# Seven block products instead of eight in 16 of the 22 pairs of the first FFN's input GEMM

## The chip, the core and the metric

The kernel runs on one core of a Trainium2 chip. The metric is device time in microseconds, the median over the runs of one kernel. TensorE does the matrix products into PSUM, VectorE (DVE) and ScalarE (ACT) work on SBUF and PSUM, GpSimd (POOL) on SBUF, SyncE (SP) issues most of the DMAs. The engines run their own queues and meet at semaphores.

## The reference

One inference step of one decoder layer: half-step SwiGLU, an attention and pooling block, half-step SwiGLU, each with adaLN modulation before it and a LayerNorm behind it. The change touches the first SwiGLU alone:

```python
def swiglu(u, w_in, w_out):
    a, b = jnp.split(u @ w_in, 2, axis=-1)
    return (jax.nn.silu(a) * b) @ w_out

def modulate(h, s):
    return h * (1.0 + scl[:, s]) + shift[:, s]

h = swiglu(modulate(x, 0), p['w_ffn1_in'], p['w_ffn1_out'])
x = layer_norm(ALPHA * x + 0.5 * gate[:, 0] * h, p['ln_gain'][0], p['ln_bias'][0])
```

The model width is 1024, the FFN width 2816, and there are 512 + 64 = 576 tokens. All is float32.

## The kernel before

**Layout.** Activations lie with features on the 128 partitions and the 576 tokens along the free axis, in 8 tiles (`XT`, the residual x; `UH` and `UL`, the modulated u). Every float32 operand is split into a high part in the matmul type fp32r (a copy on ACT) and a low part (a subtraction on DVE), and a product is three matmuls: high by high, high by low, low by high.

**The input GEMM of an FFN** makes 22 pairs of 128 columns, one of the a half and one of the b half of `w_in`. A plain pair is two chunks of 1024 x 128 weights. `product` (L344) runs one chunk: 8 feature tiles, 3 terms, 2 halves of 288 tokens, so 48 matmuls of 288 columns, and 96 a pair. ACT splits off the chunk's high part (`hi`, L259), DVE the low part (`lo`, L263), each into one of two slots; ACT takes the silu of a out of PSUM (L745), DVE multiplies by b (L763), ACT and DVE split the result into `HH` (L749) and `HL` (L769). Two chunks are on their way at a time.

**The seven-product form** is there before the change for 20 of the 22 pairs of the *second* FFN. The weights of a pair are seen as 2 x 2 blocks (a or b; lower or upper 512 features), and u as 2 x 2 blocks (lower or upper features; first or second 288 tokens). Seven products of sums of blocks replace eight. One product is 4 feature tiles, 3 terms, one half of the tokens: 12 matmuls (L1415), 84 a pair. The sums of weight blocks are four DVE subtractions and additions of 128x512 a pair (`block_s1` to `block_s4`, L1373 to L1390), the seven blocks are split by ACT (`block_hi`, L1364) and DVE (`block_lo`, L1369), and PSUM is read and added up by three ACT copies and three DVE additions a pair (L1434 to L1444, L1485 to L1493). The sums of u are made once (`factor_sums`, L1330, four instructions of 128x1152) and split once (`factor_hi` L1341, `factor_lo` L1345); two of the four split sums lie in `TB`, which shares its SBUF with `XT`, so x is spilled to DRAM (`spill`, L1532) and read back later (L991).

**What else runs in the first FFN.** The adaLN vectors of later stages are computed in five units beside the input GEMM. After each pair but the first two, TensorE runs two pieces (`ada_piece`, L1563) whose weights SP loads into `AW` (`ada_load`, L1555); a unit of eight pieces is copied out by ACT (`unit_copy`) and turned by TensorE (`unit_add`, L1577).

**Order.** Each engine's queue is written out by hand: `ffn_pe`, `ffn_act`, `ffn_dve` and `ffn_sp` in the first and second FFN. In the first, SP loads chunk after chunk, each when the slot's former chunk is split, and between them two `AW` loads a pair, each when TensorE has run the piece before the last in that buffer.

Of the kernel before, what the change touches and what calls it, by code (L numbers as in the profile page):

```python
# [7 lines left out]

# [5 lines left out]
F32 = mybir.dt.float32  # L14
# [9 lines left out]
KT = D // P  # L24
TP = 512
# [36 lines left out]
PHASES = [("setup", 0, 4, 4), ("ffn1_in", 2 * FT, FT, FT), ("ffn1_out", 3 * KT, 4, 4), ("ln0", 0, 1, 0),  # L62
# [22 lines left out]
def bucket_runs():  # L85
# [5 lines left out]
    return [int(np.argmax(b == k)) for k in range(NBKT)] + [len(b)]  # L91


def build(nc, x_prompt, x_sample, c_prompt, c_sample, cache_k_cmp, cache_v_cmp, cache_k_slc, cache_v_slc,
# [6 lines left out]
    with ExitStack() as ctx:  # L101
# [33 lines left out]
        STT = sb("STT", [TT, 9 * NT])  # L135
        ADS = RS[:, 0:2 * ACOL]
# [266 lines left out]
        def mod_buf(m, i):  # L403
            return U8[:, m, :] if i == 2 else T2[:, m % 2, :]

# [5 lines left out]
        def mod_hi(act, m, i):  # L411
            act.wait_ge(u32_ready, KT * i + m + 1)
            nc.scalar.activation(UH[:, m, :], T2[:, m % 2, :], ACT.Copy).then_inc(uh_done, 1)


        U8 = AR1[:, 8 * 2 * T:12 * 2 * T].rearrange("p (m t) -> p m t", m=KT)
# [204 lines left out]
        def ffn_pe(pe, i):  # L621
            a, b = f"ffn{i}_in", f"ffn{i}_out"

            def in_body(r, per, j0, first, unit=None):
                for j in range(j0, j0 + 4):
                    s = j % 2
                    if not first or j > 1:
                        pe.wait_ge(slot_free[s], SL0[a][s] + 1 + r * (per // 2) + j // 2)
                        if i == 2 and first and j == 2:
                            third_product(pe, a)  # L630
                            continue
                        product(pe, CH0[a] + r * per + j, (CH0[a] + j) % 2, s, 0, KT, UH, UL, True, True)
# [4 lines left out]
                    if unit is not None and s == 1:  # L637
                        k = (j - 4) % 8 - 1
                        ada_piece(pe, unit, k)
                        ada_piece(pe, unit, k + 1)  # L640
                        if k == 0 and first is None:
                            unit_add(pe, unit - 1, 5, T2[:, 1, 0:2 * P], unit * (2 * UCOL) - 2 * UCOL)
            in_body(0, 4, 0, True)
            if i == 1:
                in_body(0, 8, 4, False, 0)
                in_body(0, 8, 8, False, 0)
                with pe.Fori(1, FFN_UNITS) as r:
                    in_body(r, 8, 4, None, r)
                    in_body(r, 8, 8, False, r)
            else:  # L650
                seven_pe(pe)
                tokens_pe(pe)
                return
# [2529 lines left out]
```

## Time and profile before

| | us |
|---|---|
| median of 3 runs (1286.68 to 1290.34) | 1288.25 |
| the profiled execution, whole | 1289.31 |
| its span, first to last instruction | 1287.7 |
| TensorE busy (share of the span) | 1246.8 (97%) |
| VectorE busy | 697.8 (54%) |
| ScalarE busy | 512.5 (40%) |
| 20 pairs of the first FFN's input GEMM, pieces among them | 278.33 |
| 20 pairs of the second FFN's input GEMM (seven products) | 224.08 |

Times in the rows below are microseconds from the start of the span unless marked ns. Matmul rows overlap one another in the trace, so the mean duration of one (some 294 ns) is longer than the distance from one start to the next. That distance, a stretch of time by its count of matmuls, is what a matmul costs.

### The profile page before, as it was taken

The page shows a single profiled execution, that of the slowest core. Times are in us where ns is not written, and L with a number is a line of the kernel's source. Part 1 is how long each engine was busy: PE and PEld are TensorE (multiplying, and loading weights), DVE is VectorE, ACT ScalarE, POOL GpSimd, SP SyncE. Part 2 cuts the span into 40 slices and gives each one's busy share as a digit, 9 for nine tenths or more (in the row PEclk, how much of TensorE's full clock was granted, in tenths as well). Part 3 has the DMA queues.
Part 4 walks back from the last instruction along what each step waited for, and adds up shares of the span by engine and source line. Part 5 has one row for each costly group of instructions (what it writes and reads, how often), then busy time and mean ns, then how long its engine had stood idle before and what let it go on. Part 6 is the DMA issues. An engine that isn't in the chain of part 4 may idle for free.

```text
span 1287.7 us, 25082 instructions
## 1 busy us (share of the span) xinstructions
PE 1246.8 (97%) x9496; PEld 1116.2 (87%) x9496; DVE 697.8 (54%) x1244; ACT 512.5 (40%) x867; POOL 193.3 (15%) x379
## 2 busy tenths in 40 slices
PE   6999999999999999999989999999999999999997
PEld 3899999999899998999456666999999999978875
DVE  2522223223333357233468777578988888733466
ACT  3322222222211135343456655236556655533443
POOL 3000000000000022755085043022000000041000
PEclk9999999999999998999999999989999999999999
DMA  9535545545453224867453046623233333394463
GB/s 297 174 104 171 152 131 166 160 130 151 127 166 89 76 77 108 173 166 222 122 129 98 2 118 179 195 85 125 82 92 97 98 98 98 90 293 128 150 191 130
DMA packets 219628, 175.08 MB, mean 136 GB/s; under 512 B 47624, under 2 KB 198968, under 8 KB 219465
## 3 DMA queue, kind: packets, MB, share of 16 engines
q1 hardware_dynamic: 212641, 155.56, 41.7%
q0 software_dynamic: 6896, 18.35, 4.8%
q8 instruction: 52, 0.85, 0.3%
q14 instruction: 39, 0.32, 0.1%
HBM read 167.11 MB, written 10.99 MB: 138 GB/s over the span
## 4 chain that ended last, share of the span: by engine, by line
PE 87%; DVE 5%; ACT 4%; DMA 2%; issue 1%; DVEq 1%; SPq 0%; POOL 0%; ACTq 0%; POOLq 0%
PE ps L344 41%; PE ps L1415 16%; PE ps L1038 9%; PE ps L303 3%; PE ps L2896 2%; PE ps L2071 2%; PE ps L1563 1%; PE ps L2884 1%; ACT AR L2284 1%; DMA RAW<-in_w_ffn_out_dram 1%; PE ps L286 1%; PE ps L2088 1%; PE ps L2180 1%; PE ps L1614 1%; PE ps L425 1%
## 5 line engine op out<-in xcount | busy, mean ns | idle before, releaser
L263 DVE TENSOR_TENSOR WL<-RAW,WH 128x1024 fp32r<-128x1024 f32 x93 | 115.0, 1237 | 209.7 <-ACT WH L259 206.4
L344 PE MATMUL ps<-UH,WH 128*128 128x288 f32 x992 | 215.1, 297 | 1.0 <-DVE WL L263 1.0
L344 PE MATMUL ps<-UL,WH 128*128 128x288 f32 x992 | 210.9, 294 | 0.0
L344 PE MATMUL ps<-UH,WL 128*128 128x288 f32 x992 | 210.9, 293 | 0.0
L344 PEld LDWEIGHTS ps<-UH,WH 128*128 128x128 f32 x992 | 158.0, 188 | 7.4 <-issue 6.2
L344 PEld LDWEIGHTS ps<-UL,WH 128*128 128x128 f32 x992 | 159.4, 187 | 0.0
L344 PEld LDWEIGHTS ps<-UH,WL 128*128 128x128 f32 x992 | 158.4, 188 | 0.0
L259 ACT ACTIVATE WH<-RAW 128x1024 fp32r<-128x1024 f32 x93 | 97.9, 1054 | 143.4 <-PE ps L344 128.6
L1038 PE MATMUL ps<-WH,H 128*128 128x512 f32 x380 | 97.7, 398 | 0.8 <-ACT WH L1011 0.8
L574 POOL TENSOR_TENSOR AR<-AR 128x576 f32<-128x576 f32 x12 | 19.0, 1581 | 518.7 <-ACT AR L489 455.6
L1415 PE MATMUL ps<-TB,WH 128*128 128x288 f32 x480 | 96.8, 294 | 0.0
L1415 PE MATMUL ps<-UH,WH 128*128 128x288 f32 x320 | 94.1, 294 | 0.9 <-DVE RS L1489 0.9
L1415 PE MATMUL ps<-UL,WH 128*128 128x288 f32 x320 | 94.2, 294 | 0.0
L1415 PE MATMUL ps<-UH,WL 128*128 128x288 f32 x320 | 94.2, 294 | 0.0
L1038 PEld LDWEIGHTS ps<-WH,H 128*128 128x128 f32 x380 | 70.2, 188 | 18.4 <-ACT WH L1011 1.5
L1415 PEld LDWEIGHTS ps<-TB,WH 128*128 128x128 f32 x480 | 77.0, 187 | 0.0
L344 PE MATMUL ps<-HH,WH 128*128 128x288 f32 x338 | 72.2, 294 | 1.7 <-DVE HL L769 1.7
L344 PE MATMUL ps<-HL,WH 128*128 128x288 f32 x338 | 72.3, 294 | 0.0
L344 PE MATMUL ps<-HH,WL 128*128 128x288 f32 x338 | 72.0, 294 | 0.0
L1415 PE MATMUL ps<-TB,WL 128*128 128x288 f32 x240 | 70.9, 295 | 0.0
L1019 DVE TENSOR_TENSOR WL<-RAW,WH 128x1024 fp32r<-128x1024 f32 x28 | 34.9, 1247 | 50.5 <-ACT WH L1011 50.4
L1415 PEld LDWEIGHTS ps<-UH,WH 128*128 128x128 f32 x320 | 60.1, 188 | 1.1 <-DVE WL L1369 1.1
(445 smaller groups left out, 2335.0 us busy)
## 6 DMA issues: line engine op xcount, KB each, us to landing
RAW<-in_w_ffn_in_dram SPq DMA_DIRECT2D x58, 512.0 KB, 5.7
AW<-in_w_ada_dram SPq DMA_DIRECT2D x42, 512.0 KB, 4.3
RAW<-in_w_ffn_out_dram SPq DMA_DIRECT2D x36, 512.0 KB, 3.7
RAW<-in_w_ffn_in_dram SPq DMA_DIRECT2D x40, 256.0 KB, 2.9
AR<-in_w_ada_dram SPq DMA_DIRECT2D x7, 1024.0 KB, 11.4
RAW<-in_w_ffn_out_dram SPq DMA_DIRECT2D x16, 448.0 KB, 3.7
AR<-in_w_ada_dram SPq DMA_DIRECT2D x14, 512.0 KB, 5.9
RAW<-in_w_in_dram SPq DMA_DIRECT2D x28, 256.0 KB, 3.8
```

The source lines that it names most:

```text
L259: nc.scalar.activation(WH[:, slot, :], RAW[:, slot, :], ACT.Copy).then_inc(hi_done, 1)
L263: nc.vector.tensor_tensor(WL[:, slot, :], RAW[:, slot, :], WH[:, slot, :].bitcast(F32), ALU.subtract).then_inc(split_done, 1)
L286: mm = nc.tensor.matmul(ps[:, h, 0:HT], THIRD[ph][:, at + k * P:at + (k + 1) * P], R[:, k, h * HT:(h + 1) * HT], start=(k == 0 and q == 0) ...
L303: mm = nc.tensor.matmul(ps[:, 2 * s + h, 0:HT], W[:, w, k * P:(k + 1) * P], R[:, k, h * HT:(h + 1) * HT], start=(k == 0 and q == 0 and s n ...
L344: mm = nc.tensor.matmul(ps[:, 2 * uslot + h, 0:HT], W[:, wslot, k * P:(k + 1) * P], R[:, k0 + k, h * HT:(h + 1) * HT], start=(first and k ...
L425: mm = nc.tensor.matmul(ps[0:TT, bank, col + j:col + j + 1], src[:, j * TT:(j + 1) * TT], ONE[:, 0:1], start=True, stop=True)
L574: a = nc.gpsimd.tensor_tensor(sq[:, 0, :], sq[:, 0, :], sq[:, m, :], ALU.add)
L1019: nc.vector.tensor_tensor(WL[:, n % 2, :], raw_at(j)[0], WH[:, n % 2, :].bitcast(F32), ALU.subtract).then_inc(split_done, 1)
L1038: mm = nc.tensor.matmul(out, src, moving(h), start=(k == 0 and q == 0), stop=(k == FT - 1 and q == 2))
L1415: mm = nc.tensor.matmul(acc(bank), W[g % 4][:, k * P:(k + 1) * P], R[:, k, :], start=(k == 0 and q == 0 and i in (0, 1, 3)), stop=(k == HK ...
L2071: mm = nc.tensor.transpose(ps[:, 4 + g, k * P:(k + 1) * P], X[xslot(u, 2 * br + g)][:, k * P:(k + 1) * P], IDN[:, :])
L2896: mm = nc.tensor.matmul(ps[64 * g:64 * g + 64, 4 + kv, 0:NB * CS], WPHI[:, kv, l, :], KT8[kv][:, g, :, l % 8, l // 8:l // 8 + CS], start=( ...
```

## The change

Pairs 2 to 17 of the first FFN take the seven-product form; pairs 0 and 1, and 18 to 21, stay plain. The code of the second FFN becomes a form for both, with a record (`Seven`) of where each finds its buffers and counts.

- The modulated x, in float32, is no longer in a two-deep buffer (`T2`) but kept whole (`U1`), over the rows of x that have been turned already. The sums of u are made from it.
- x is spilled to DRAM as the stage begins and read back in its last four pairs.
- The split sums lie in `TB`, in parts of `HH` and `HL` that are filled last (18 to 21, hence 16 pairs), and in a new tile `FACX` of 128 x 1152.
- TensorE's two pieces follow each pair of seven products as they followed each plain pair. The unit's copy goes to `RS`, since `T2` holds block sums.
- ACT and DVE have the 16 pairs written out, in place of loops.

The core of the diff:

```diff
+        N1, N2 = 16, 20
+        SEVEN = (Seven(ffn=1, n=N1, ..., ring=0, raw=1, banks=((0, 1, 4), (2, 3, 7)),
+                       wb=(halves(RAW[:, 0, :]), halves(AR1[:, AR1N - WCH:AR1N])), xs=T2[:, 1, 0:BLK], u=U1,
...
         def mod_dve(m, i):
-            buf = T2[:, m % 2, :]
-            if m >= 2:
-                nc.vector.wait_ge(u_split, KT * UCNT[i] + m - 1)
+            buf = U1[:, m, :]
...
         def ffn_pe(pe, i):
-            if i == 1:
-                in_body(0, 8, 4, False, 0)
-                in_body(0, 8, 8, False, 0)
-                with pe.Fori(1, FFN_UNITS) as r:
-                    in_body(r, 8, 4, None, r)
-                    in_body(r, 8, 8, False, r)
+            in_body(0, True)
+            seven_pe(pe, SEVEN[i - 1])
...
+            pe.wait_ge(st_h, SEVEN[0].n - 1)
+            pe.wait_ge(st_sum, 3 * SEVEN[0].n - 3)
+            in_body(4, False)
+            in_body(8, False)
...
         def seven_pe(pe, V):
...
+                    if V.ffn == 1:
+                        unit_pieces(pe, r, p, not first)
...
         def ffn_sp(sp, i, w1, w2):
             if i == 1:
                 for j in range(2, 4):
-                    ffn_in_load(sp, 1, 0, 4, j, w1)
-                with sp.Fori(0, FFN_UNITS) as r:
-                    for j in range(4, 12):
-                        ffn_in_load(sp, 1, r, 8, j, w1)
-                        if j % 2 == 1:
-                            for k in (j - 5, j - 4):
-                                ada_load(sp, r, k)
+                    ffn_in_load(sp, 1, j, w1)
+                for s in range(2):
+                    sp.wait_ge(slot_free[s], 1 + KT // 2)
+                for k in range(2):
+                    ada_load(sp, 0, k)
+                for m in range(KT):
+                    sp.dma_start(XSP[:, m, :], XT[:, m, :]).then_inc(xsp, 16)
+                load_wb(sp, V, 1)
+                sp.wait_ge(split_done, CH0[a] + 5)
+                load_wb(sp, V, 0)
+                sp.wait_ge(split_done, CH0[a] + 6)
+                load_wa(sp, V, 0, 0)
+                load_wa(sp, V, 0, 1)
+                seven_sp(sp, V)
+                sp.wait_ge(st_split, 7 * V.n - 7)
+                ffn_in_load(sp, 1, 4, w1)
+                for k in range(6, 8):
+                    ada_load(sp, FFN_UNITS - 2, k)
+                sp.wait_ge(st_split, 7 * V.n - 1)
+                for j in range(5, 12):
+                    ffn_in_load(sp, 1, j, w1)
+                    if j % 2 == 1:
+                        for k in (j - 5, j - 4):
+                            ada_load(sp, FFN_UNITS - 1, k)
+                    if j == 5:
+                        sp.wait_ge(st_mm, 7 * V.n - 2)
+                    if j < 9:
+                        for m in (2 * j - 10, 2 * j - 9):
+                            sp.dma_start(XT[:, m, :], XSP[:, m, :]).then_inc(xsp, 16)
...
         def seven_sp(sp, V):
             for p in range(1, V.n):
+                q = V.done + p
+                sp.wait_ge(st_s13, 2 * q)
+                sp.wait_ge(st_s24, 2 * q - 1)
+                load_wa(sp, V, p, 0)
+                sp.wait_ge(st_split, 7 * q - 1)
+                load_wa(sp, V, p, 1)
+                if p + 1 < V.n:
+                    sp.wait_ge(st_split, 7 * q)
+                    load_wb(sp, V, p + 1)
+                if V.ffn == 1 and p + 1 < V.n:
+                    for k in (2 * (p % UNROLL), 2 * (p % UNROLL) + 1):
+                        ada_load(sp, p // UNROLL, k)
```

DVE's queue as the stage opens, before: the low part of the first FFN's third chunk stands right behind the last low parts of u.

```order
L408 TENSOR_TENSOR UL<-T,UH 128x576 [waits uh_done] x2
L263 TENSOR_TENSOR WL<-RAW,WH 128x1024 [waits hi_done]
L763 TENSOR_TENSOR T<-MU,ps 128x576 [waits hl_done,chunk_mm,slot_free0]
L769 TENSOR_TENSOR HL<-T,HH 128x576 [waits hh_done]
L263 TENSOR_TENSOR WL<-RAW,WH 128x1024 [waits hi_done] x2
```

The same place after; L1403 makes the sums of u, L1423 their low parts, L1466, L1471 and L1453 the sums of weight blocks, L1448 the low parts of blocks.

```order
L429 TENSOR_TENSOR UL<-AR,UH 128x576 [waits uh_done] x2
L1403 TENSOR_TENSOR AR<-AR 128x1152 x2
L286 TENSOR_TENSOR WL<-RAW,WH 128x1024 [waits hi_done]
L779 TENSOR_TENSOR T<-MU,ps 128x576 [waits hl_done,chunk_mm,slot_free0]
L286 TENSOR_TENSOR WL<-RAW,WH 128x1024 [waits hi_done]
L784 TENSOR_TENSOR HL<-T,HH 128x576 [waits hh_done]
L1403 TENSOR_TENSOR AR<-AR 128x1152 [waits tf_made] x2
L1423 TENSOR_TENSOR HH<-AR,HH 128x1152 [waits tb_hi]
L1466 TENSOR_TENSOR T<-RAW 128x512 [waits apre_full5]
L1471 TENSOR_TENSOR RAW<-RAW 128x512 [waits apre_full3]
L1448 TENSOR_TENSOR WL<-RAW,WH 128x512 [waits st_hi]
```

Two sums of u now stand ahead of the third chunk's low part, and two more sums, a low part and two block sums ahead of the first block's.

SP's queue at the same place, before: a loop of two chunk loads and two `AW` loads a pair (the bare `ISA` rows are its waits).

```order
L2961 DMA AW<-in_w_ada_dram 128x8x256
L240 DMA RAW<-in_w_ffn_in_dram 128x8x128 [waits split_done] x2
L862 UNCONDITIONAL_BRANCH
L862 ISA
L240 ISA [waits split_done]
L240 DMA RAW<-in_w_ffn_in_dram 128x8x128
L238 REGISTER_ALU
L240 ISA [waits split_done]
L240 DMA RAW<-in_w_ffn_in_dram 128x8x128
L1554 REGISTER_ALU
L1555 ISA [waits ada_mm]
L1555 DMA AW<-in_w_ada_dram 128x1024
```

And after (L1648 loads `AW`, L900 spills x, L1617 loads half an a chunk, L1621 a whole b chunk):

```order
L3055 DMA AW<-in_w_ada_dram 128x8x256
L263 DMA RAW<-in_w_ffn_in_dram 128x8x128 [waits split_done] x2
L1648 DMA AW<-in_w_ada_dram 128x1024 [waits ada_mm,slot_free1,slot_free0]
L1648 DMA AW<-in_w_ada_dram 128x1024 [waits ada_mm]
L900 DMA x_spill_dram<-XT 128x576 x8
L1621 DMA AR<-in_w_ffn_in_dram 128x8x128
L1621 DMA RAW<-in_w_ffn_in_dram 128x8x128 [waits split_done]
L1617 DMA RAW<-in_w_ffn_in_dram 128x4x128 [waits split_done]
L1617 DMA RAW<-in_w_ffn_in_dram 128x4x128
L1617 DMA RAW<-in_w_ffn_in_dram 128x4x128 [waits st_s24,st_s13]
L1617 DMA RAW<-in_w_ffn_in_dram 128x4x128 [waits st_split]
L1621 DMA RAW<-in_w_ffn_in_dram 128x8x128 [waits st_split]
```

The first loads of the seven-product stage stand behind two `AW` loads and the eight spills; from the second pair on, two `AW` loads that wait for TensorE's pieces (`ada_mm`) stand ahead of the next pair's first half chunk.

## Rows read from the trace of the kernel before

**Rows 1.** The page: busy time of each engine, share of the span, instructions.
```profile
span 1287.7 us, 25082 instructions
PE 1246.8 (97%) x9496; PEld 1116.2 (87%) x9496; DVE 697.8 (54%) x1244; ACT 512.5 (40%) x867; POOL 193.3 (15%) x379
```

**Rows 2.** Groups of PE: line, op, out<-in, shape, count, busy us, mean ns, idle before.
```profile
L344 PE MATMUL ps<-UH,WH 128*128 128x288 f32 x992 | 215.1, 297 | 1.0 <-DVE WL L263 1.0
...
L1415 PE MATMUL ps<-UH,WH 128*128 128x288 f32 x320 | 94.1, 294 | 0.9 <-DVE RS L1489 0.9
```

**Rows 3.** Windows: stretch, length, busy of PE, PEld, DVE, ACT, POOL, clock, DMA share, GB/s.
```profile
67.27:345.60 278.33, 278.33 (x2245) 264.00 (x2245) 79.27 (x80) 66.61 (x84) 0.00 (x0) 1.00 0.49 147
902.22:1126.30 224.08, 223.14 (x1684) 222.93 (x1683) 195.00 (x358) 133.77 (x260) 0.00 (x0) 1.00 0.33 94
```

**Rows 4.** Chain that ended last: start, length, what.
```profile
54.38 25.62 PE ps L344 x192
80.00 1.00 PE ps L1563 x16
81.00 12.89 PE ps L344 x96
...
912.99 205.44 PE ps L1415 x1548
```

**Rows 5.** Timeline of DVE as the first FFN opens: start, length, [idle before <-releaser].
```profile
49.59 1.60 DVE L408 TENSOR_TENSOR UL<-T,UH 128x576 fp32r<-128x576 f32 x2
53.01 1.22 DVE L263 TENSOR_TENSOR WL<-RAW,WH 128x1024 fp32r<-128x1024 f32 x1 [1.82 <-ACT WH L259]
```

**Rows 6.** Timeline of DVE and PE in the second FFN's opening.
```profile
887.57 2.62 DVE L1330 TENSOR_TENSOR AR<-AR 128x1152 f32<-128x1152 f32 x2
...
904.49 1.35 DVE L1345 TENSOR_TENSOR TB<-AR,TB 128x1152 fp32r<-128x1152 f32 x1
905.76 0.69 DVE L1369 TENSOR_TENSOR WL<-RAW,WH 128x512 fp32r<-128x512 f32 x1
...
912.39 0.45 DVE L1489 TENSOR_TENSOR RS<-RS,ps 128x288 f32<-128x288 f32 x1
```

**Rows 7.** Timeline of PE there.
```profile
912.99 0.37 PE L1415 MATMUL ps<-UH,WH 128*128 128x288 f32 x1 [0.94 <-DVE RS L1489]
```

**Rows 8.** Timeline of SP's DMA issues, first FFN's opening and the spill before the second.
```profile
31.51 26.87 SPq L240 DMA_DIRECT2D RAW<-in_w_ffn_in_dram  x4
58.64 1.08 SPq L1555 DMA_DIRECT2D AW<-in_w_ada_dram  x2
...
868.76 14.90 SPq L1532 DMA_DIRECT2D x_spill_dram<-XT  x8
```

**Rows 9.** The page's DMA issues: queue, count, KB each, us from issue to landing.
```profile
AW<-in_w_ada_dram SPq DMA_DIRECT2D x42, 512.0 KB, 4.3
RAW<-in_w_ffn_in_dram SPq DMA_DIRECT2D x40, 256.0 KB, 2.9
```

**Rows 10.** Windows as in rows 3: idle queue at the opening, mixed load and read-back, a slow-clock stretch.
```profile
46.00:50.00 4.00, 4.00 (x32) 3.95 (x32) 2.58 (x10) 1.25 (x3) 0.00 (x0) 1.00 0.00 0
864.00:868.00 4.00, 4.00 (x23) 3.20 (x23) 2.93 (x11) 1.36 (x2) 0.00 (x0) 0.50 0.72 214
1142.00:1156.00 14.00, 13.92 (x60) 11.25 (x61) 6.12 (x5) 4.28 (x5) 0.00 (x0) 1.00 0.97 322
```

**Rows 11.** Timeline of the setup's last adaLN products, which release `AW`.
```profile
44.77 1.05 PE L1637 MATMUL ps<-AW,CT 128*32 128x256 f32 x16
```

**Rows 12.** Waits in the second FFN's steady pairs: who, for whom, us in total, times, longest.
```profile
ACT WH L1364 <- DVE T L1373: 26.7, 18, 1.5
DVE WL L1369 <- ACT WH L1364: 20.9, 68, 0.3
```

More of the change, by code:

```diff
@@ L7 @@
 from contextlib import ExitStack
+from dataclasses import dataclass
 import numpy as np
@@ L24 @@
 KT = D // P
+HK = KT // 2
 TP = 512
@@ L91, in bucket_runs @@
     return [int(np.argmax(b == k)) for k in range(NBKT)] + [len(b)]
+@dataclass
+class Seven:
+    ffn: int
+    n: int
+    done: int
+    wa0: int
+    wb0: int
+    x0: int
+    ring: int
+    raw: int
+    banks: tuple
+    wb: tuple
+    xs: object
+    u: object
+    tf: object
+    fac1: tuple
+    fac4: tuple
 def build(nc, x_prompt, x_sample, c_prompt, c_sample, cache_k_cmp, cache_v_cmp, cache_k_slc, cache_v_slc,
@@ L788, in ffn_dve @@
[L788 to L801 removed]
+                factor_sums(V, 2, 3)
@@ new lines, in ffn_dve @@
+            block_lo(dve, V, 0, 1)
+            block_s2(dve, V, 0)
+            factor_lo(dve, V, 1)
+            factor_lo(dve, V, 2)
+            in_product(dve, 1, a, 3)
+            block_lo(dve, V, 0, 2)
+            block_lo(dve, V, 0, 3)
+            block_lo(dve, V, 0, 4)
+            block_s4(dve, V, 0)
+            in_low(dve, 1, 1)
+            seven_dve(dve, V)
+            for j in range(4, 12):
+                lo(dve, *split_args(*next_chunk(a, j))[:2])
+                if j % 2 == 1:
+                    in_product(dve, 1, a, j)
+                    in_low(dve, 1, pair_of(j))
@@ L1300, in blocks @@
+        def blocks(ar, first):
             flat = ar[:, :, :].rearrange("p s n -> p (s n)")
-            return [flat[:, ((q // 2 + RC) % 2) * WCH + (q % 2) * BLK:][:, 0:BLK] for q in range(4)]
-        WHB, WLB = blocks(WH), blocks(WL)
+            return [flat[:, ((q // 2 + first) % 2) * WCH + (q % 2) * BLK:][:, 0:BLK] for q in range(4)]
+        WHB, WLB = ([blocks(ar, V.ring) for V in SEVEN] for ar in (WH, WL))
+        RBLK = [halves(RAW[:, V.raw, :]) for V in SEVEN]
         tf_made, tb_hi, tb_split = sem("tf_made"), sem("tb_hi"), sem("tb_split")
-        LANDED = 16 + 16 * NPG
@@ L1470, in seven_dve @@
+                    act.wait_ge(st_h2, q)
+                    f = SP_F0 + p - 1
+                    dst = HH[:, f, :] if V.ffn == 1 else H2[:, f, 0:T]
+                    nc.scalar.activation(dst, EVH, ACT.Copy).then_inc(hh_done, 1)
+        def seven_dve(dve, V):
+            a, mm0, sm0 = f"ffn{V.ffn}_in", 7 * V.done, 3 * V.done
+            for t in range(7 * V.n + 1):
                 p, i = t // 7, t % 7
-                nxt = t + 3 < 7 * SP_N
+                q = V.done + p
+                nxt = t + 3 < 7 * V.n
```

587 lines of the change are left out of this document (297 added, 290 removed).

## The prediction

> **What bounds the kernel now.** I read the page's busy times first: TensorE is busy 97% of the span, VectorE 54%, ScalarE 40% [rows 1]. A busy PE is not yet a full one, so I then asked what PE waited for in the two FFN stages. In the groups of PE, the plain product (L344) has 1.0 us of idle time in front of 992 matmuls of one kind, the seven-product one (L1415) 0.9 us in front of 320 [rows 2]. The windows say the same: from 67.27 to 345.60 us, 20 pairs of the first FFN, PE is busy for all of 278.33 us at the full clock (1.00, so 2.4 GHz), while DVE works 79.27 and ACT 66.61 us [rows 3]. The stage is bound by the number of matmuls, and the helpers have room. So the saving is counted in matmuls, and the rest of the work is to find where the new form makes PE wait.
>
> **What a matmul costs.** The chain has 192 plain matmuls in 25.62 us, 0.1334 us each [rows 4]. The second FFN's 20 seven-product pairs take 224.08 us with one wait of 0.94 us in them: 223.14 / 1680 = 0.1328 us [rows 3, 7]. The two forms pay the same for a matmul, although the plain one runs each weight tile twice in a row and the other once. The Trainium skill ("TensorE: Matmul & The Clock Gate", Back-to-back issue gap) gives N/2.4 + 2.5 ns for one matmul, 122.5 ns at 288 columns. The trace disagrees, 133 ns; by the page's figure the next term would be an estimated 23.5 us.
>
> **Removed: 12 matmuls a pair.** 96 - 84 = 12, times 0.1334, is 1.60 us; 16 pairs make **-25.6 us**. Taken pair against pair it is 25.62 / 2 - 223.14 / 20 = 12.81 - 11.16 = 1.65, or -26.4. I take the first, since the shorter pair of the second FFN has no pieces after which PE starts anew (12.89 for the pair behind the pieces, against 12.81) [rows 4]. The pieces (1.00 us a pair) and the units' turns stay where they are, between pairs. A pair in the loop takes 278.33 / 20 = 13.92 us now and 12.3 after.
>
> **Helpers in steady pairs: nothing on the path.** The form asks DVE for 195.00 / 20 = 9.75 us a pair and ACT for 133.77 / 20 = 6.69 [rows 3]. In the second FFN that fits into 11.2 us without PE waiting; DVE's own waits there are short ones for ACT (0.3 us at the longest) [rows 12]. Here a pair has 12.3 us, DVE comes to 79%, and only `unit_copy` is new on ACT. The cover is 1.1 us better than where it already holds. If it were gone, each pair would lose what it is late.
>
> **SP's queue in steady pairs.** The next pair's first half chunk now stands behind two `AW` loads, which wait for the pieces of the pair before. Let a pair's first product start at T. The pieces end at T - 0.6 and T - 0.1, so the `AW` loads leave then and the half chunk at about T + 0.3. An `AW` load lands in 4.3 us and a half chunk in 2.9 [rows 9]; together with the two ahead of it (1.3 MB; at 214 to 322 GB/s [rows 10] 4.1 to 6.1 us) it lands by T + 3.5 to T + 5.5. DVE wants it for a block sum at about T + 6, behind four products' worth of work, and PE for the next pair at T + 12.3. Cost 0; PE has some 5 us in hand after the split (0.6 + 0.7 us, twice at most).
>
> **The opening, three terms.** (1) Two sums of u (2.62 us for two [rows 6]) now stand on DVE ahead of the third chunk's low part. DVE ends the low parts of u at 49.59 + 1.60 = 51.19 and idles until 53.01 for ACT [rows 5]. Of 2.62 us, 1.82 fall into this gap; the rest, **+0.8 us**, is on the path, since PE waits for this very instruction already (1.0 us) [rows 2]. (2) The first half chunk must come before about 62 us. `AW` is released at 44.77 + about 0.6 [rows 11], so its loads leave at about 45.4, 13 us earlier than now (58.64) [rows 8], onto an idle queue (0 GB/s from 46 to 50) [rows 10]. Behind them go 8 spills of 288 KB, two b chunks and the half chunk: 4.7 MB. At 322 GB/s, the rate of a stretch with weight loads and x read back [rows 10], they land by 60.1; at 214, the rate where spills begin, by 67.5. PE is done with the plain chunks at 55.2 + 12.8 = 68.0. The first rate costs nothing; by the second the first product starts 1 us late and DVE's queue behind it drags on, some 3 us in all. I take 0. (3) In the second FFN PE waits 0.94 us in its first pair [rows 7], for the middle addition at 912.39 [rows 6]: DVE had the split sums (1.35 us each), the blocks and the plain pair's end to do at once. Here one of these split sums is done before the first product, but ACT's block for it comes no earlier. Going down DVE's new list with these durations I find that addition ending at T + 10.0 where PE wants it at T + 9.6. Bounds 0 and 0.94, taken **+0.5 us**.
>
> **The close: nothing.** Chunk 4 is asked for in the last pair but one, and its split (1.0 + 1.2 us) starts when the last but two products is done, 3.2 us before the last ends, with 1.1 us of pieces behind it. The next chunk has 6.4 us more. Reading x back puts 2.4 MB among 4 MB of weights and 4 MB of `AW` loads in some 55 us, under 200 GB/s, where 322 have been seen [rows 10].
>
> **The sum.** -25.6 + 0.8 + 0 + 0.5 = -24.3 us. Against the profiled execution's 1289.31 that is 1265.0. This execution stands 1.06 us above the median of 1288.25, so the median after should be **1264.0 us**, 1.9% less. What a measurement of this kernel can tell from no change is about 0.3%, 4 us.
>
> **Rival 1: the opening chokes on the spill.** SP's single queue carries the 8 spills ahead of what PE needs next, and writing may be slower than reading. At half of 322 GB/s, 4.7 MB take 29 us, to 74.6; with split and DVE's list behind it PE loses 7 to 9 us, and, as the stretch at half clock (0.50) shows after a thin stretch of PE work [rows 10], perhaps 2 us more at 1.2 GHz. The time would be 1271 to 1275. For it: nothing in this trace has 8 spills at once; those seen came 1.9 us apart [rows 8]. Against: the idle queue and the 13 us of lead. The Trainium skill ("DMA: Bandwidth & Descriptors", Queues, rings and completion order) says that each DMA engine takes descriptors in ring order, which is what makes the spills stand ahead; what it would cost is the number above. Chance 14%.
>
> **Rival 2: a wait in every pair.** DVE and ACT pass blocks back and forth (26.7 us of ACT waiting for DVE in 18 pairs) [rows 12], now with other PSUM banks and the pieces between. If each pair lost 0.3 to 0.6 us, the time would be 1269 to 1274. Chance 8%.
>
> **Rival 3, the other side: the half chunk comes too late each time.** The mechanism is the SP order above: the `AW` loads wait for TensorE, the half chunk for them, and the next pair for the half chunk. It decides from a landing 5 us later than T + 5.5; from 6.6 us later (1.6 us a pair) the kernel is slower than before, at 8 us later 1288 + 16 x 1.4 - 1.5 = 1309. Loads that land 12 us after their issue would be needed; with a queue of 1.3 MB none of the kind is in the rows. Chance 2%.
>
> **Rival 4: the form saves less than it says**, because PE restarts cost more between short products. 7 waits a pair are there in the second FFN and cost nothing. Chance 4%, 1266 to 1270.
>
> **How the numbers follow.** The forecast, 1261.5 to 1268 with the bounds of its terms (-26.4 and no stall; 214 GB/s), has 72%. Up to 1273 the range takes in most of rivals 1 and 2 and leaves out some 12%. Faster by over 0.3% is 96%, within 0.3% is 2%, slower 2%.
>
> **What would show it.** In the trace after: 16 x 84 matmuls of the new form at 0.133 us from one start to the next; pairs of 12.3 us; the first plain chunk of `product` starting near 55.2 instead of 54.38; the eight spills leaving between 46 and 50 us and the first half chunk landing before 62; one wait of PE of about half a microsecond in the first pair, for DVE's middle addition; no wait for DVE or a load at the pair borders; the later stages unchanged but 24 us earlier. A wait at each border, or PE idle for more than 2 us between 55 and 85 us, would prove it wrong.

## The result, and the profile after

The changed kernel takes **1267.01 us** (median of 4 runs, 1266.38 to 1268.61), the kernel before beside it 1289.30 us (4 runs, 1286.68 to 1290.98): ratio **0.983**, 95% interval 0.981 to 0.985. Two further sets of runs of the same two kernels gave 1266.99 against 1290.07 and 1265.35 against 1290.92 us. Forecast were 1264.0 against a base of 1288.25, a ratio of 0.981. So the mechanism holds and the gain is 22 to 26 us where 24.3 were forecast. The profiled executions, which can be taken apart, are 22.9 us apart: 1289.31 before, 1266.38 after.

The page of the kernel after, against [rows 1]:

```profile
span 1264.4 us, 25031 instructions
PE 1221.5 (97%) x9304; PEld 1091.1 (86%) x9304; DVE 801.0 (63%) x1460; ACT 572.5 (45%) x1015; POOL 193.9 (15%) x379
```

192 matmuls fewer, which is 16 x 12, and DVE with 103 us more work than before. PE is as full as it was. The groups of PE, as in [rows 2], have idle times of 1.6, 0.9 and 0.4 us and no other in front of the products of the two input GEMMs:

```profile
L1500 PE MATMUL ps<-UH,WH 128*128 128x288 f32 x512 | 152.2, 297 | 0.9 <-DVE RS L1588 0.9
...
L367 PE MATMUL ps<-UH,WH 128*128 128x288 f32 x480 | 103.9, 297 | 1.6 <-DVE WL L286 1.6
...
L1500 PE MATMUL ps<-FACX,WH 128*128 128x288 f32 x64 | 18.9, 295 | 0.4 <-DVE RS L1588 0.4
```

The chain of work that ended last shows the stage pair by pair, as in [rows 4]. L367 is `product` now, L1500 the seven-product matmul, L1656 the adaLN pieces between the pairs:

```profile
55.84 12.95 PE ps L367 x96
...
78.69 1.82 PE ps L1500 x12
80.51 1.00 PE ps L1656 x16
81.51 11.32 PE ps L1500 x84
...
325.38 104.98 PE ps L367 x792
```

A seven-product pair behind pieces is 11.32 us, where a plain one was 12.89 [rows 4]; with the pieces 12.32. The windows of the first pair, of the 15 pairs that follow and of the plain pairs at the end (columns as in [rows 3]):

```profile
68.79:80.51 11.72, 11.36 (x88) 10.99 (x91) 11.04 (x18) 7.51 (x14) 0.00 (x0) 1.00 0.25 72
80.51:266.69 186.18, 186.18 (x1517) 174.98 (x1520) 144.97 (x251) 101.90 (x198) 0.00 (x0) 1.00 0.53 167
267.69:325.38 57.69, 56.00 (x453) 52.95 (x453) 16.95 (x20) 15.32 (x20) 0.00 (x0) 1.00 0.64 194
```

Over 15 pairs PE has not one gap, although DVE is busy 145 of 186 us (78%). The first pair has 0.36 us of idle time. The 57.69 us at the end hold the same code as before, between 290.64 and 348.32 in the kernel before 57.68.

**Where the 22.9 us come from** (23.3 of the span), by the start of the same instruction in the two traces. The third chunk's product starts 1.46 us later (54.38 [rows 4], 55.84). From there to the first product of the output GEMM before had 293.94 us, after 269.54: the stage is **24.40 us** shorter. From there to PE's wait in the second FFN's first pair it is 564.67 and 565.12 us, 0.45 more. The rest of the span is 0.8 us shorter, since one wait of PE of 0.8 us in the last stage is not there in this execution. 1.46 - 24.40 + 0.45 - 0.8 = -23.3 us of span.

### The profile page after: what moved, and what is told of

Same layout as the page of the kernel before. It is cut to its first block, busy times and chain, and to the rows that moved or that the text cites. A ratio compares the mean times of both kernels' runs of the same rounds, so it can differ in the third digit from the quotient of the medians.

```text
span 1264.4 us, 25031 instructions
## 1 busy us (share of the span) xinstructions
PE 1221.5 (97%) x9304; PEld 1091.1 (86%) x9304; DVE 801.0 (63%) x1460; ACT 572.5 (45%) x1015; POOL 193.9 (15%) x379
## 4 chain that ended last, share of the span: by engine, by line
PE 86%; DVE 6%; ACT 4%; issue 1%; DMA 1%; DVEq 1%; SPq 0%; POOL 0%; ACTq 0%; POOLq 0%
PE ps L1500 30%; PE ps L367 26%; PE ps L1101 11%; PE ps L326 3%; PE ps L2990 2%; ACT AR L2378 2%; PE ps L1656 2%; PE ps L2978 1%; PE ps L2165 1%; PE ps L309 1%; PE ps L1708 1%; DVE AR L2548 1%; PE ps L2274 1%; PE ps L2182 1%; PE ps L447 1%
## 5 line engine op out<-in xcount | busy, mean ns | idle before, releaser
L1500 PE MATMUL ps<-UH,WH 128*128 128x288 f32 x512 | 152.2, 297 | 0.9 <-DVE RS L1588 0.9
L1500 PE MATMUL ps<-UH,WL 128*128 128x288 f32 x512 | 150.9, 295 | 0.0
L1500 PE MATMUL ps<-UL,WH 128*128 128x288 f32 x512 | 150.6, 294 | 0.0
L286 DVE TENSOR_TENSOR WL<-RAW,WH 128x1024 fp32r<-128x1024 f32 x61 | 76.2, 1250 | 114.6 <-ACT WH L282 112.5
L1500 PE MATMUL ps<-TB,WH 128*128 128x288 f32 x736 | 148.7, 294 | 0.0
L1500 PEld LDWEIGHTS ps<-TB,WH 128*128 128x128 f32 x736 | 118.1, 188 | 0.0
L1448 DVE TENSOR_TENSOR WL<-RAW,WH 128x512 fp32r<-128x512 f32 x144 | 99.1, 688 | 28.5 <-ACT WH L1443 28.4
L1500 PE MATMUL ps<-TB,WL 128*128 128x288 f32 x368 | 108.7, 295 | 0.0
L367 PE MATMUL ps<-UH,WH 128*128 128x288 f32 x480 | 103.9, 297 | 1.6 <-DVE WL L286 1.6
L1443 ACT ACTIVATE WH<-RAW 128x512 fp32r<-128x512 f32 x144 | 90.3, 627 | 29.0 <-PE ps L1500 24.2
L367 PE MATMUL ps<-UH,WL 128*128 128x288 f32 x480 | 102.2, 294 | 0.0
L367 PE MATMUL ps<-UL,WH 128*128 128x288 f32 x480 | 102.2, 294 | 0.0
L1500 PEld LDWEIGHTS ps<-UH,WH 128*128 128x128 f32 x512 | 96.1, 188 | 6.1 <-DVE T L1575 3.7
L1500 PEld LDWEIGHTS ps<-UL,WH 128*128 128x128 f32 x512 | 96.1, 188 | 0.0
L1500 PEld LDWEIGHTS ps<-UH,WL 128*128 128x128 f32 x512 | 96.1, 188 | 0.0
L367 PEld LDWEIGHTS ps<-UH,WH 128*128 128x128 f32 x480 | 76.5, 188 | 3.0 <-issue 2.6
L367 PEld LDWEIGHTS ps<-UL,WH 128*128 128x128 f32 x480 | 77.0, 187 | 0.0
L367 PEld LDWEIGHTS ps<-UH,WL 128*128 128x128 f32 x480 | 76.7, 188 | 0.0
```

Source lines behind the costliest of these rows:

```text
L286: nc.vector.tensor_tensor(WL[:, slot, :], RAW[:, slot, :], WH[:, slot, :].bitcast(F32), ALU.subtract).then_inc(split_done, 1)
L367: mm = nc.tensor.matmul(ps[:, 2 * uslot + h, 0:HT], W[:, wslot, k * P:(k + 1) * P], R[:, k0 + k, h * HT:(h + 1) * HT], start=(first and k ...
L1443: nc.scalar.activation(WHB[V.ffn - 1][g % 4], block_raw(V, p, i), ACT.Copy).then_inc(st_hi, 1)
L1448: nc.vector.tensor_tensor(WLB[V.ffn - 1][g % 4], block_raw(V, p, i), WHB[V.ffn - 1][g % 4].bitcast(F32), ALU.subtract).then_inc(st_split, 1)
L1500: mm = nc.tensor.matmul(acc(bank), W[g % 4][:, k * P:(k + 1) * P], R[:, k, :], start=(k == 0 and z == 0 and i in (0, 1, 3)), stop=(k == HK ...
```

## The experiments

They are told by the question that they answer; all but two_terms (one term of each product left out) and extra_matmuls (some products counted twice) compute what the reference does. "The stage" is the time from the third chunk's first product to the first of the output GEMM, 269.54 us in the first trace of the changed kernel. It is compared rather than the span, since in the kernels that have one and the same code up to there, the third chunk's product starts anywhere between 54.70 and 56.44 us.

### Is the saving the matmuls, and nothing else?

**The same kernel again.**

> The changed kernel once more, to be compared with the others on one chip. All theories: about 1266 us in the profiled execution, 22 to 24 us under the kernel before; the pairs of seven products 12.3 us from one start to the next (84 matmuls in 11.3 and 1.0 for the pieces).

1266.99 us, ratio 0.9825 (0.980 to 0.985). Its stage is 325.16 - 55.62 = 269.54 us, the same to 0.01 us as in the first trace.

**Twelve pairs in the new form in place of 16.**

```diff
-        N1, N2 = 16, 20
+        N1, N2 = 12, 20
```

with eight plain pairs behind them instead of four.

> Seven products in 12 of the 22 pairs of the first FFN instead of 16, eight plain pairs behind them instead of four; the rest as in the changed kernel. If the gain is 12 matmuls a pair and the opening's cost is paid once, the time rises by 4 x 1.57 = 6.3 us over the changed kernel (12.89 us of matmuls in a plain pair, 11.32 in the other). If a good part of the loss against the plain sum came from something that grows with the number of pairs, the rise is below 5 us; if the transition costs more than the trace shows, it is above 7.

1273.03 us, ratio 0.9872 (0.985 to 0.989), 6.0 us above the changed kernel. The border between the forms in the chain:

```profile
205.86 11.32 PE ps L1500 x84
218.18 12.89 PE ps L367 x96
```

The stage is 331.87 - 56.05 = 275.82 us, 6.28 more: four times 1.57. The saving is in proportion to the pairs.

**The seventh product twice.** The pairs of the first FFN have 96 matmuls again, with all of the new form's work for DVE, ACT and SP.

```diff
-                        for k in range(HK):
+                        for k in [*range(HK)] * (2 if V.ffn == 1 and i == 6 else 1):
```

> In the first FFN the seventh product of every pair is run twice (its sum is then wrong, nothing else is changed), so that TensorE has 96 matmuls a pair as in the plain form, and ACT, DVE and SP all the work of the seven-product form. If only the number of matmuls matters and the helpers cost TensorE nothing, each pair takes 12.9 us and the pieces, and the time is that of the changed kernel + 16 x 1.60 = +25.6 us, that is 1 to 2 us above the kernel before. If the seven-product form gains by anything else, or loses by its helpers, the difference is not 25.6 but less or more by over 2 us.

1292.99 us, ratio 1.0027 (1.0002 to 1.0053), 26.0 us above the changed kernel. Its pairs in the chain:

```profile
83.36 12.90 PE ps L1500 x96
97.27 12.91 PE ps L1500 x96
```

With 96 matmuls a pair of the new form lasts as long as a plain one (12.89), and the gain is gone altogether. So the count of matmuls is the whole of the gain, and the new form's other work costs nothing in a steady pair. In all it costs some 2 us in this run: the stage is 351.03 - 55.41 = 295.62 us, 1.68 more than before the change (293.94), and the sums of u come on top with 0.55 (below). The 2.9 us between the medians are near what can be told from nothing. 26.08 us above the changed kernel's stage are a little more than 16 x 1.57, mostly because the first pair waits 1.05 us here where it waits 0.36 there; *The spill earlier* comes back to that.

### How much room do the helpers have?

**56 matmuls a pair**: high weights by low activations is left out of the first FFN's seven products.

```diff
                             for z, (W, R) in enumerate(((whb, rh), (whb, rl), (wlb, rh))):
+                                if V.ffn == 1 and z == 1:
+                                    continue
```

> In the first FFN's seven products the term high weights by low activations is left out (8 matmuls a product instead of 12, 56 a pair; the output loses that part). TensorE then needs 56 x 0.133 = 7.5 us and 1.0 for the pieces, 8.5 us a pair. If the helpers have the room that their busy times say (DVE 9.0 us of busy time a pair, with ends that overlap), they become the bound and a pair takes 8.7 to 9.7 us. If the hand-over between ACT, DVE and TensorE is already nearly as long as the pair, it stays above 11 us.

1236.58 us. The pairs are some 10.2 us, not 8.5 (56 x 0.1334 + 1.0). A window over a dozen pairs, and PE's waits in it (who, for whom, us in total, times, longest):

```profile
82.00:230.00 148.00, 134.38 (x1056) 116.68 (x1049) 135.82 (x244) 92.03 (x190) 0.00 (x0) 0.99 0.67 205
```

```profile
ACT WH L1443 <- DVE T L1453: 20.8, 14, 1.5
PE ps L1502 <- DVE RS L1590: 13.3, 14, 2.9
ACT WH L1443 <- DMA RAW<-in_w_ffn_in_dram: 12.2, 13, 2.9
```

DVE is busy 92% and PE waits in each pair for the middle addition (L1590 here, L1588 in the changed kernel): DVE's work with its hand-overs to ACT, and the half chunk's landing, do not go below 10.2 us. That lies between the two outcomes of the expectation (8.7 to 9.7, or above 11). Against 12.3 it leaves some 2 us a pair.

### What does the opening cost, and why?

**The sums of u later.** The two sums stand on DVE behind the third chunk's low part.

```diff
-            factor_sums(V, 0, 2)
             lo(dve, *split_args(a, 2)[:2])
...
             in_low(dve, 1, 0)
+            factor_sums(V, 0, 2)
             factor_sums(V, 2, 4)
```

> The two sums of u that stand ahead of the third chunk's low part on DVE are moved behind the fourth chunk's. By the theory (they cost 0.55 us at this place and nothing elsewhere), TensorE starts the third chunk 1.0 us after it is out of work, as in the kernel before, instead of 1.55, and DVE's later list still ends in time; the first pair of seven products keeps its wait of 0.3 to 0.5 us. If the sums only moved the lateness, the first seven-product pair waits longer by what the third chunk gains.

One run of 1265.91 us. PE's wait for the third chunk is 1.00 us again, as before the change [rows 2], against 1.55 in the changed kernel: so the sums on the path cost 0.55 us. But the stage is 325.66 - 54.87 = 270.79 us, 1.25 more: PE now waits 1.04 us for the middle addition in the first pair, where it had waited 0.36, and another 0.31 us for ACT earlier in the same pair. The work was not saved by moving it, only paid later; net it loses 0.7 us, and the total, which seems to say the opposite, is the setup's chance.

**The spill earlier**: the eight spills leave SP ahead of the `AW` loads, with a semaphore of their own.

```diff
+                for m in range(KT):
+                    sp.dma_start(XSP[:, m, :], XT[:, m, :]).then_inc(xsp1, 16)
                 for k in range(2):
                     ada_load(sp, 0, k)
-                for m in range(KT):
-                    sp.dma_start(XSP[:, m, :], XT[:, m, :]).then_inc(xsp, 16)
```

> The eight spills are issued before the two AW loads, which wait for the setup's last products, and count on a semaphore of their own. The first half chunk should land 2 to 4 us earlier and DVE's wait for it (1.2 us) go. TensorE's time should not change (within 0.2 us at the first product of the stage), since DVE is on time there without it; if the load's wait was part of the path, the first pair's wait of 0.4 us goes too.

One run of 1266.26 us. DVE's wait for the half chunk, 1.22 us in the changed kernel, is gone, and the stage is 324.56 - 55.01 = 269.55 us, no shorter at all. In the first pair PE waits 0.35 us as it did. In the changed kernel DVE's wait for the load lies in its slack: with the load early DVE idles 0.64 us instead, up to 68.03, 0.07 us after TensorE's last plain product of the opening ends, and only there the list that leads to the middle addition begins.

The slack was nearly used up, though, and extra_matmuls, which runs the same instructions up to there, shows the edge. First the changed kernel, where T, the end of the plain products, is 68.79, then extra_matmuls, where it is 68.36:

```profile
63.93 0.69 DVE L1471 TENSOR_TENSOR RAW<-RAW 128x512 f32<-128x512 f32 x1 [1.22 <-DMA RAW<-in_w_ffn_in_dram]
78.69 0.37 PE L1500 MATMUL ps<-FACX,WH 128*128 128x288 f32 x1 [0.36 <-DVE RS L1588]
```

```profile
64.25 0.69 DVE L1471 TENSOR_TENSOR RAW<-RAW 128x512 f32<-128x512 f32 x1 [1.51 <-DMA RAW<-in_w_ffn_in_dram]
78.95 0.37 PE L1500 MATMUL ps<-FACX,WH 128*128 128x288 f32 x1 [1.05 <-DVE RS L1588]
```

A landing at T - 4.9 us cost nothing, one at T - 4.1 cost 0.7. In the other traces with these sums ahead of the third chunk (double_spill and two_terms apart) DVE had the half chunk at T - 4.9 or before, and the wait is 0.35 to 0.38 us.

**The spill twice**, eight more writes of 288 KB into a second buffer, waited for as the first.

```diff
                 for m in range(KT):
+                    sp.dma_start(XSP2[:, m, :], XT[:, m, :]).then_inc(xsp2, 16)
+                for m in range(KT):
                     sp.dma_start(XSP[:, m, :], XT[:, m, :]).then_inc(xsp, 16)
```

> x is spilled twice as the stage opens, to two places in DRAM: 16 spills of 288 KB instead of 8, ahead of the first loads of the seven-product stage, and ACT waits for both. If the queue is what those loads wait behind, 2.36 MB more at about 350 GB/s shift the first half chunk by 6 to 8 us, from 63.9 to about 71, and TensorE stands still for 3 to 6 us before or in the first pair. If the spill is hidden anyway (rival), TensorE's waits stay at 0.4 us.

1273.47 us, one run. DVE and PE in its timeline, and the window of the first pair:

```profile
68.39 0.69 DVE L1472 TENSOR_TENSOR T<-RAW 128x512 f32<-128x512 f32 x1 [6.29 <-DMA RAW<-in_w_ffn_in_dram]
...
70.55 0.41 PE L1506 MATMUL ps<-UH,WH 128*128 128x288 f32 x1 [1.77 <-DVE WL L1454]
```

```profile
70.55:86.65 16.10, 14.39 (x101) 13.22 (x101) 15.24 (x23) 10.24 (x18) 0.00 (x0) 0.89 0.23 67
```

The half chunk lands at 69.1 in place of 63.9 us. The first product starts 1.8 us late, but the stage is 5.13 us longer (330.52 - 55.85 = 274.67): DVE, which had idled 6.3 us for the b chunk on the same queue (L1472 is the first block sum), then works through its list almost in one piece (15.24 of 16.10 us), and PE stands idle another 1.7 us, at a mean clock of 0.89. That mean is a fall to the lower level: PE had been idle for 1.77 us up to 70.55, and from 71.72 to 75.13 us the granted clock is 0.50 (1.2 GHz), with matmuls 0.24 us apart in place of 0.13. So the first 24 take 4.99 us where 24 x 0.134 are 3.2. A late start of 1.75, 1.35 more waiting than in the changed kernel and 1.8 for these 24 are 4.9 of the 5.13 us. That is rival 1, made to happen, with the "perhaps 2 us more at 1.2 GHz": it takes 2.3 MB more on the queue. Another 2 us of its 7 stand behind the stage, where nothing was changed: 1.45 between the output GEMM and the second FFN's first pair and 0.5 after it. They stay unexplained; one_copy (below) has 1.0 us more at the first of these places as well.

**All three at once**, and the low part of the second plain chunk's result (`in_low`, 0.75 us) moved behind the middle addition in both FFNs.

```diff
-                in_low(dve, 2, 1)
...
-            in_low(dve, 1, 1)
             seven_dve(dve, V)
...
                     nc.vector.tensor_tensor(EVP, EVP, acc(V.banks[p % 2][0]), ALU.add).then_inc(st_sum, 1)
+                    if p == 0:
+                        in_low(dve, V.ffn, 1)
```

> The changed kernel with three moves in its openings, nothing left out: the eight spills leave SP ahead of the AW loads; the two sums of u stand on DVE behind the third chunk's low part and the low part of the first half chunk's chunk; and in both FFNs the low part of the plain chunk that follows the seven-product opening (in_low for chunk 1) stands behind the middle addition of the first pair. Theory (DVE's queue in the first pair is what makes PE wait, and nothing else is late): the third chunk's wait falls from 1.55 to 1.0 us, the first-pair waits of 0.36 us (first FFN) and 0.93 us (second) go, so 1.3 to 1.9 us less in all and a profiled time of about 1265, with the setup's own spread of up to 0.9 us on top. Rival A (moving the sums alone cost 1.2 us in the first pair, since it put DVE behind for all that follows): the early spill does not give that back, the third chunk gains 0.55 us and the first pair loses about 1 us, and only the second FFN's 0.9 us remains as gain: 1266 to 1267. Rival B: the low part that was moved is now late itself and PE waits at the border of the first and second pair.

1266.26 us, ratio 0.982 (0.979 to 0.985), beside 1265.35 us of the changed kernel in the same set of runs: no gain. The stage is 324.22 - 53.48 = 270.74 us, as with the sums alone: the first half of rival A. Its other half, a gain of 0.9 us in the second FFN, did not come: the second FFN, where the moved low part was meant to take the wait of 0.93 us away, has it still:

```profile
887.43 0.37 PE L1499 MATMUL ps<-UH,WH 128*128 128x288 f32 x1 [0.94 <-DVE RS L1587]
```

DVE's timeline there tells why, first of the changed kernel, then of this one:

```profile
883.88 0.68 DVE L1459 TENSOR_TENSOR RAW<-RAW,T 128x512 f32<-128x512 f32 x1
884.48 0.22 DVE L786 TENSOR_TENSOR H<-T,H 128x64 fp32r<-128x64 f32 x1
884.62 0.68 DVE L787 TENSOR_TENSOR H<-T,H 128x512 fp32r<-128x512 f32 x1
885.26 0.69 DVE L1448 TENSOR_TENSOR WL<-RAW,WH 128x512 fp32r<-128x512 f32 x1
```

```profile
880.80 0.69 DVE L1458 TENSOR_TENSOR RAW<-RAW,T 128x512 f32<-128x512 f32 x1
882.19 0.69 DVE L1447 TENSOR_TENSOR WL<-RAW,WH 128x512 fp32r<-128x512 f32 x1 [0.70 <-ACT WH L1442]
```

The low part had filled the 0.7 us in which ACT turns DVE's block difference into its high part. With it gone DVE waits out the same 0.7 us. No label says this in the changed kernel, because a gap that is filled leaves no idle time behind.

### How near is the late half chunk?

The prediction held that a half chunk may land 5 us later than T + 5.5 (T is the start of the pair before the one it serves) before a pair is longer.

**Two copies of 512 KB, DRAM to DRAM, ahead of the half chunk in each pair.**

```diff
                 sp.wait_ge(st_s24, 2 * q - 1)
+                if V.ffn == 1:
+                    for k in range(2):
+                        sp.dma_start(DUM[2 * p + k], w_ada[0, k * P:(k + 1) * P, 0:D]).then_inc(dum, 16)
                 load_wa(sp, V, p, 0)
```

> Ahead of each of the pairs' first half chunks two more copies of 512 KB (DRAM to DRAM, of no use) stand on SP's queue, behind the two AW loads: some 1.0 MB more that goes through the DMA engines per pair, and reads and writes both in DRAM. The half chunk lands 3 to 5 us later. By my reckoning TensorE has 5 us in hand there, so nothing or less than 0.5 us a pair is lost. If the order of SP's queue is the danger that the third rival says, each pair takes 1 us or more longer and the time rises by over 15 us.

1286.71 us: almost all of the gain is lost, 1.3 us a pair (the stage is 344.48 - 55.55 = 288.93 us), and the expectation was wrong. The chain through one pair, with T = 122.65, the end of the pieces (L1632 are the copies):

```profile
121.65 1.04 PE ps L1661 x16
...
123.21 0.50 SPq L1632
...
124.79 6.67 DMA RAW<-in_w_ffn_in_dram
...
131.48 0.04 DVE AR L1473
...
132.46 0.68 DVE WL L1450
133.14 0.38 DVE RS L1590
133.52 0.04 issue
133.56 1.85 PE ps L1502 x12
```

The half chunk lands at T + 8.8 us, some 3.2 later than usual: it leaves at T + 2.1 in place of T + 0.6, since SP has the copies to issue, and takes 6.7 us in place of 5.1. DVE wants it for `block_s3`, a block difference for the next pair, and this stands in its queue ahead of two additions and a low part of the pair at hand. 2.06 us after the landing the middle addition is done, and PE, which starts 0.04 us later in this pair (0.14 in others), has waited 1.16 us for it, since T + 9.75. So the deadline is not the next pair's first product, T + 12.3, but T + 9.75 - 0.14 - 2.06 to T + 9.75 - 0.04 - 2.06, about **T + 7.6**. The pair is 12.76 us (to 135.41) where 11.32 is usual: the wait, and 0.24 us by which the twelve matmuls behind it take 1.85 and not 12 x 0.134 us.

**The same copies behind the half chunk**: the two statements change places.

> As the run with two copies of 512 KB in every pair of the first FFN, the same bytes, but the copies stand on SP behind the first half chunk and not ahead of it. Theory (the order on the queue did the damage: with the copies ahead the half chunk landed 8.8 us after the pair's start where DVE can use it until about 7.7): the half chunk lands at about T + 5 to T + 6 again, pairs return to 12.3 us, and the time is 1267 to 1268. Rival (the added traffic itself slows the loads, whatever stands where): pairs of 13 to 13.7 us and 1278 to 1286.

1266.97 us, one run; the stage is 325.98 - 56.44 = 269.54 us, that of the changed kernel to 0.01 us. The half chunk lands between T + 4.8 and T + 7.0. The same bytes in the same pairs cost nothing. It is the order on the queue and not the traffic.

**One copy ahead.**

> One copy of 512 KB ahead of the half chunk in place of two. Two copies brought its landing from T + 5.1 to T + 8.8 us and cost 1.2 to 1.4 us a pair; by the time from that landing to the end of the middle addition (2.06 us) and the time at which PE wants that addition (T + 9.8) it is free up to T + 7.7. One copy should land it at about T + 6.9: no wait of PE, 1267 to 1268. By my prediction's reckoning (5 us in hand) two copies would have been free as well, which they were not. Rival (what decides is DVE's wait for the sum at T + 6.1, passed on in full): 0.8 us a pair, about 1279.

1267.86 us, one run; the stage is 325.39 - 54.70 = 270.69 us, 1.15 more. It is not spread over the pairs: three of them are 0.48, 0.34 and 0.30 us too long, and the others last as long as ever. The chain of the first of the three, with T = 105.01:

```profile
104.01 1.05 PE ps L1661 x16
...
106.94 5.86 DMA RAW<-in_w_ffn_in_dram
...
114.48 0.37 DVE RS L1590
114.85 0.14 issue
114.99 1.82 PE ps L1502 x12
```

It lands at T + 7.8 and the pair is 11.80 us, 0.48 too long. In the other two it lands at T + 7.7. In the next pair (T = 117.81) the half chunk lands at T + 7.3, and that pair has its 11.32 us. Every other pair, with landings up to T + 7.4, is as long as in the changed kernel. The edge lies between T + 7.4 and T + 7.7, where the run with two copies put it. The expectation had a landing at about T + 6.9 and no cost; the landings came later, and the cost is small.

**The changed kernel a third time**, beside these.

> The changed kernel itself, beside the kernel before and the run above on one chip: 1266.4 to 1267.5 us, ratio 0.982 to 0.983. How far its setup (first plain chunk of the product at 55.84 us in the first trace of it) differs from one execution to the next says how much of the 0.9 us by which the setup was later than before belongs to the change; by the theory that it is chance, some execution of the changed kernel starts it at or below 55.2 us.

1265.35 us (1263.93 to 1269.84), ratio 0.981 (0.978 to 0.984); the stage is 325.46 - 55.88 = 269.58 us. The setup of this one is no earlier than in the first trace, so that half of its expectation did not come true in it. But one_copy, whose code is the same up to there, starts the third chunk at 54.70 us, and extra_behind at 56.44.

## Why the prediction was right, and where it was off

**Removed matmuls: right, 0.5 us too high.** "12 times 0.1334 is 1.60 us" a pair; measured are 12.89 - 11.32 = 1.57 us. The prediction had 0.1334 from plain pairs; a pair of the new form runs at 11.32 / 84 = 0.1348 us a matmul, with the restart behind the pieces in it, and 12.89 / 96 = 0.1343 is the plain one's. The removed twelve are the difference of the two, 0.131 each. 16 x 1.57 = 25.1, not 25.6. Whether the 0.03 us a pair are rival 4's restarts between shorter products was not tested; in all they are 0.5 us. By the figure of the Trainium skill ("TensorE: Matmul & The Clock Gate", Back-to-back issue gap) that the prediction set beside the rows, which the page gives for a single matmul by itself, an estimated 122.5 ns, it would have been 23.5 us; this trace and extra_matmuls (26 us for 192 matmuls, 0.135 each) go with the rows.

**Steady pairs: right.** No wait in 15 pairs, and DVE at 78% where 79% was said. Rival 2 is out. two_terms shows what the cover is worth: the helpers would carry pairs of 10.2 us.

**Opening, term 1 (+0.8): right in kind, measured +0.55.** PE's wait is 1.55 us in place of 1.00 [rows 2], with DVE as follows, against [rows 5]:

```profile
51.94 2.62 DVE L1403 TENSOR_TENSOR AR<-AR 128x1152 f32<-128x1152 f32 x2
54.48 1.22 DVE L286 TENSOR_TENSOR WL<-RAW,WH 128x1024 fp32r<-128x1024 f32 x1
```

The gap had been 1.82 us of idle time by the row, and I had counted durations end to end. Back to back, DVE's instructions overlap by 0.08 us at each seam (51.94 + 2.62 = 54.56, but the next starts at 54.48), which is most of the 0.25.

**Opening, term 2 (0): right, with the arrival later than said.** The half chunk landed at 63.9 us, inside 60.1 to 67.5 but beyond the 62 that I called needed, and DVE waited 1.22 us for it. early_spill shows that this wait costs nothing, and extra_matmuls that it was close: by T - 4.1 the half chunk is late there. So the 62 us, 6 us ahead of the plain chunks' end at 68.0, were 1 to 2 us too strict, and the margin that was left was under 1 us. While the spills were under way the rate was above the 322 GB/s I had reckoned with: 354 from 50 to 54 us, 389 from 54 to 58. But from 46 to 50 it was 161 and from 58 to 62 297, and over the whole way from 46.4 to 63.9 us 285. What took time at the start is SP's queue:

```profile
46.43 0.83 SPq L1648 DMA_DIRECT2D AW<-in_w_ada_dram  x2
47.30 6.58 SPq L900 DMA_DIRECT2D x_spill_dram<-XT  x8
53.92 0.78 SPq L1621 DMA_DIRECT2D AR<-in_w_ffn_in_dram  x1
55.73 0.38 SPq L1621 DMA_DIRECT2D RAW<-in_w_ffn_in_dram  x1
57.53 17.00 SPq L1617 DMA_DIRECT2D RAW<-in_w_ffn_in_dram  x4
```

The first `AW` load leaves 1.0 us later than the 45.4 I had put. The eight spills leave 0.82 us apart, not "between 46 and 50 us", and the loads behind them wait for buffers as well; the half chunk leaves at 57.5 and takes 6.4 us to land, where the median of its kind is 3.0.

**Opening, term 3 (+0.5): measured 0.36.** The middle addition ends at T + 9.8 and not T + 10.0, PE wants it at T + 9.5 and not T + 9.6 (T = 68.79):

```profile
78.18 0.38 DVE RS L1588
78.55 0.14 issue
78.69 1.82 PE ps L1500 x12
```

The cause was half wrong. Among the things that DVE had "to do at once" I named the plain pair's end; combo moved that away, and PE waited as long as it did without that move (1.05 us against 1.04 in sums_later, and 0.94 against 0.93 in the second FFN). What is left are the split sums, 1.35 us each, which were not varied, and ACT: in the chain the first 4.6 us from T, to 73.44, are all ACT's (high parts of blocks, of the plain pair's result and of a split sum, and copies out of PSUM), and only then comes DVE's part of the list.

**SP's order in steady pairs: the cost (0) was right, the margin wrong.** The half chunk lands at T + 5.0 to T + 6.1 in the changed kernel (with T = 118.47 it leaves at 119.0 and takes 5.1 us), at the late end of "T + 3.5 to T + 5.5" and beyond it. The step that fails is "PE has some 5 us in hand": it looked at the next pair's need for the data, and not at what stands in DVE's queue behind the instruction that waits for it. In hand are 7.6 - 6.1 to 7.6 - 5.0, so 1.5 to 2.6 us. With that rival 3 decides from a landing at T + 7.6 and not T + 10.5. A landing at T + 8.8 cost 1.44 us, so the kernel would be slower than before from about T + 9 on, not from T + 12.1. It never came near that by itself; but two copies of 512 KB were enough to bring it there.

**The close and the later stages: right.** The plain pairs at the end take 57.69 us, 57.68 before.

**What was not in the sum.** The setup's end, 0.9 us later in the profiled execution (1.46 less the 0.55), and 0.45 us in attention. Both are in code that the change leaves alone, and both vary as much between executions of one code: setups that end between 54.70 and 56.44, attention stretches of 564.10, 564.75 and 565.12 us in the three traces of the changed kernel. They are chance as far as these runs can tell; the trace of before is a single one, and whether a part of the 0.9 belongs to the change can't be said from it.

So the forecast of -24.3 us stands against -24.40 (stage) + 0.55 (sums) = **-23.85 us** for what the change does, and -22.9 with this pair's chance. In the stage -25.1 for the matmuls, 0.36 for the first pair's wait and 0.2 for the slower twelve behind it make -24.5. That the sum came so near is in part luck: the matmuls gave 0.5 us less than forecast and the opening cost 0.2 us less (0.55 + 0.36 + 0.2 against 0.8 + 0.5), which partly cancel, and with the half chunk 0.8 us later against T (extra_matmuls) the first pair's wait was 0.7 us longer. The forecast median of 1264.0 was 3 us lower than what was measured, of which about 1 us is the base: 1288.25 was the median of 3 runs, and those beside the later runs were 1289.3 to 1290.9. Of the other 2 us 0.45 are the difference from 24.3 to 23.85; the rest is what these medians differ by in any case (gains of 22.3, 23.1 and 25.6 us in the three sets). The lower end of the forecast, 1261.5, lies 1.2 us below what the bounds that it names add up to (1288.25 - 26.4 + 0.8 = 1262.7); nothing hangs on it.

## What to carry to other kernels

Count what the bounding engine is relieved of, and look for the price in the first round of a loop, where the work of two stages meets; there single microseconds are found, and moving one of them elsewhere in a full queue gives it back later. A load's deadline is set by whatever stands in the queue behind the instruction that waits for it, which may belong to the pair at hand though the data belong to the next. To see the room that a steady state has, put the same extra bytes ahead of a load and then behind it: the difference is order, the rest is traffic. And compare stages between fixed instructions, not whole runs, when one or two microseconds are at stake.

## What the runs showed of the hardware beyond what was expected

- The stage of 269.5 us, in which matmuls follow one another almost without a gap, is the same to 0.04 us in three executions of the changed kernel (269.54, 269.54, 269.58), while the setup before it, which waits for the first loads, ends anywhere within 1.7 us (54.70 to 56.44 in kernels with the same code up to there).
- Writing x out and reading weights at once ran at 354 GB/s from 50 to 54 us and 389 from 54 to 58 (407 there with the double spill), against 322 in the rows of before.
- With eight spills in a row SP issued one every 0.70 to 0.82 us (5.63 us for eight in one_copy, 6.58 in the changed kernel); the two `AW` loads ahead of them took 0.83 us together.
- PE's idle stretch of 1.77 us in double_spill was followed by a fall of the granted clock to 0.50 from 71.72 to 75.13 us, with matmuls 0.24 us apart; behind the idle stretch of 1.55 us in the changed kernel, 54.29 to 55.84, the clock stays at 1.00.
- A wait costs PE more than its length: the twelve matmuls behind one took 1.82 to 1.85 us where 12 x 0.134 are 1.61.
- 1 MB of copies in each pair, behind the load that mattered, cost TensorE nothing.
